# Mean and variance of seven of nine token blocks moved from VectorE to ScalarE in the last superblock of a hybrid decoder step

## The chip, the cores and the metric

The kernel runs on one core of a Trainium2 chip. The metric is the device time of one execution in microseconds (us); for the kernel before it is the median of three runs. A profile of one further execution gives the times of the single instructions. TensorE (PE), VectorE (DVE), ScalarE (ACT), GpSimd (POOL) and SyncE (SP) each work through a queue of their own, in order, and meet through semaphores.

## The reference

One inference step of a two-layer decoder for 1024 prompt tokens and 64 new tokens, with 1024 features. Layer 0 mixes by sliding-window attention and a gated convolution, layer 1 by pooling and dilated attention. Behind each mixer and each squared-ReLU MLP stands a residual layer norm. What the change touches is the last line of it, the norm behind the MLP of layer 1, whose result is the output y:

```python
def layer_norm(x, g, b):
    xf = x.astype(jnp.float32)
    mu = jnp.mean(xf, axis=-1, keepdims=True)
    var = jnp.mean(jnp.square(xf - mu), axis=-1, keepdims=True)
    return ((xf - mu) * lax.rsqrt(var + LN_EPS) * g.astype(jnp.float32) + b.astype(jnp.float32)).astype(x.dtype)

def squared_relu_mlp(x, w1, w2):
    return jnp.square(jax.nn.relu(x @ w1)) @ w2
...
        x = layer_norm(DEEPNORM_ALPHA * x + squared_relu_mlp(x, mlp_w1[layer], mlp_w2[layer]),
                       ln2_g[layer], ln2_b[layer])
```

## The kernel before, in words

The 1088 tokens lie in nine blocks of 128 rows (the ninth, block 8, has the 64 new tokens), and XT[:, t, :] holds the 1024 features of block t. Matmuls are done on values split into a high and a low part, three matmuls for each product. The MLP runs in eight pieces of 512 hidden features. A piece computes its hidden features (matmuls of L1463, then Relu, Square and Copy on ScalarE, L760 to L766), and then a "superblock" of the down product: `row_super` on TensorE (L1494) and `sums` on VectorE (L1129), which adds each finished half block from PSUM to XT. The superblock of the last piece of a layer is also the one whose sums are followed by the layer norm; its number is R = 19 for the end of the kernel, and it is the only one that the change touches.

**TensorE's order.** `row_super` goes through five sets of blocks: (0, 1), (2, 3), (8), (4, 5), (6, 7). A unit is one half of one block: 512 features in one PSUM bank. Four chunks k of the hidden features are summed; k is the outer loop and the units of a set the inner one, so that all four units of a set end close together. A unit has 12 matmuls; those of block 8 have 8. Before the first matmul of a unit TensorE waits until VectorE has emptied the unit's bank (`r_evac`). Behind the set (4, 5) stand the matmuls of L1546, which add up the two halves of block 8 (with SEL), and wait for its sums.

**VectorE's order** is written out by hand in `norm_super` (L1145): the sums of a set, then `ln_stats` (L952) for its blocks, and so on in NORM_ORDER = (0, 1, 2, 3, 4, 5, 8, 6, 7): sums of (0, 1); norms 0, 1; sums of (2, 3); norms 2, 3; sums of (8) and (4, 5); norms 4, 5; the two copies of L1166 for block 8; sums of (6, 7); norms of 8, 6 and 7. The position p in NORM_ORDER is what the code counts by.

**One norm** in this superblock is, on VectorE, two bn_stats (L958, L959) and a bn_aggr (L960) for mean and variance; a pass over the block, (x - mean) * gain (L965); four instructions on one column, which turn the root into its refined reciprocal (L968 to L974); and a second pass, x * 1/std + bias (L980). ScalarE only takes the root of the variance (`ln_root`, L654 to L658) while VectorE does L965. SP stores a block when its second pass is done (L546).

What comes next on VectorE's queue always stands behind the norm in front of it: there is one queue.

Of the kernel before, what the change touches and what calls it, by code (L numbers as in the profile page):

```python
# [67 lines left out]
U_OIN = U_EOUT  # L68
U_OOUT = U_OIN + 3 * ODD_IN + 12
H_UNITS = 12 * N_HB  # L70

ROW_BASE = [0]
for _r in range(20):
# [21 lines left out]
def build(nc, io):  # L95
# [3 lines left out]
    with ctx:  # L99
        place = [nc.sbuf_base + (-nc.sbuf_base) % 64]  # L100

        def at(name, shape, dtype, offset):
            return nc.alloc_sbuf_tensor_at(name, shape, dtype, offset=offset)
# [6 lines left out]
        def small(name, shape):  # L110
            n = 4
            for s in shape[1:]:
                n *= s
            return at(name, shape, F32, room(n))
# [69 lines left out]
        BNS = small("BNS", [P, 12])  # L184
        MV = small("MV", [P, 2, 2])
        NM = small("NM", [P, 2])
        EPSC = small("EPSC", [P, 1])
        SD = small("SD", [P, 2])
        RS = small("RS", [P, 2])
# [24 lines left out]
        def sem(name):  # L214
            return ctx.enter_context(nc.semaphore(name))
# [3 lines left out]
        xr_in = [sem(f"xr_in{q}") for q in range(5)]  # L219
        x0_in = [sem(f"x0_in{q}") for q in range(5)]  # L220
        tables_in, tables_used, y_ready = sem("tables_in"), sem("tables_used"), sem("y_ready")
        r_mm, r_evac, w_free, packed = sem("r_mm"), sem("r_evac"), sem("w_free"), sem("packed")
        spilled = sem("spilled")
        ident_in, cols_in, kct_in, biasa_in = sem("ident_in"), sem("cols_in"), sem("kct_in"), sem("biasa_in")
# [35 lines left out]
        def turned_back(l, g, k):  # L260

            c = k % ring(l, g)
            return XR[:, c, 0:GROUP[g][1]] if c < 2 else RT[:, c - 2, 0:GROUP[g][1]]

        def rows_of(t):

            return NS if t == N_TILES - 1 else P

        def sums_of(R, t):

            q = [t in tiles for tiles in TILE_SETS].index(True)
            if t == N_TILES - 1:
                return ROW_BASE[R] + 16
            return ROW_BASE[R] + row_units(R, q)[-1][0] + 1

        def row_units(R, q):

            first = SET_UNIT[q] + (2 if R in NORM_SUPER and q == 4 else 0)
            return [(first + 2 * i + n, t, n) for i, t in enumerate(TILE_SETS[q]) for n in range(2)]
# [324 lines left out]
        def _(act):  # L604
# [49 lines left out]
            def ln_root(l, p):  # L654
                n, r = 9 * l + p, rows_of(NORM_ORDER[p])
                act.wait_ge(mv_ready, n + 1)
                act.activation(SD[0:r, n % 2:n % 2 + 1], MV[0:r, n % 2, 1:2], ACT.Sqrt,  # L657
                               bias=EPSC[0:r, :]).then_inc(std_ready, 1)  # L658

# [123 lines left out]
            def mlp(l, name, out):  # L783
                ln_super(2 * l)
                hidden_super(l, 0, 2 * l, (name, out, N_HB - 1))
                with act.Fori(0, N_HB - 1) as i:
                    hidden_super(l, i + 1, None, (name, out, i))
# [106 lines left out]
            act.wait_ge(pt_evac, len(turn))  # L894
            split_high(2, Y, (0, 1, 2), (1,))
            mlp(1, "cache_d_v", "d_vs")
            for p in range(9):
                ln_root(3, p)


        @block.vector
        def _(dve):
# [3 lines left out]
            def link(ins):  # L906

                links[0] += 1
                ins.then_inc(dve_link, 1)
                dve.wait_ge(dve_link, links[0])  # L910
# [41 lines left out]
            def ln_stats(l, p):  # L952
                n, t = 9 * l + p, NORM_ORDER[p]
                r, e = rows_of(t), slice(n % 2, n % 2 + 1)
                dve.wait_ge(r_evac, sums_of(NORM_SUPER[l], t))
                if n >= 2:
                    dve.wait_ge(zn_ready, min(n - 1, 27))
                dve.bn_stats(BNS[0:r, 0:6], XT[0:r, t, 0:512])  # L958
                link(dve.bn_stats(BNS[0:r, 6:12], XT[0:r, t, 512:1024]))  # L959
                dve.bn_aggr(MV[0:r, n % 2, :], BNS[0:r, :]).then_inc(mv_ready, 1)  # L960
                if l == 3:
                    if p == 0:
                        dve.wait_ge(tables_in, 16 * 10)
                    dve.wait_ge(mv_ready, n + 1)
                    link(dve.scalar_tensor_tensor(out=XT[0:r, t, :], in0=XT[0:r, t, :], scalar=MV[0:r, n % 2, 0:1],  # L965
                                                  in1=TG[0:r, 0, :], op0=ALU.subtract, op1=ALU.mult))
                dve.wait_ge(std_ready, n + 1)
                link(dve.reciprocal(RS[0:r, e], SD[0:r, e]))  # L968

                link(dve.scalar_tensor_tensor(out=NW[0:r, e], in0=MV[0:r, n % 2, 1:2], scalar=EPS, in1=RS[0:r, e],  # L970
                                              op0=ALU.add, op1=ALU.mult))
                link(dve.scalar_tensor_tensor(out=NW[0:r, e], in0=NW[0:r, e], scalar=-0.5, in1=RS[0:r, e],
                                              op0=ALU.mult, op1=ALU.mult))
                link(dve.scalar_tensor_tensor(out=RS[0:r, e], in0=NW[0:r, e], scalar=1.5, in1=RS[0:r, e],  # L974
                                              op0=ALU.add, op1=ALU.mult))
                if l < 3:
                    dve.scalar_tensor_tensor(out=NM[0:r, e], in0=MV[0:r, n % 2, 0:1], scalar=-1.0, in1=RS[0:r, e],
                                             op0=ALU.mult, op1=ALU.mult).then_inc(rs_ready, 1)
                else:
                    dve.scalar_tensor_tensor(out=XT[0:r, t, :], in0=XT[0:r, t, :], scalar=RS[0:r, e], in1=TG[0:r, 1, :],  # L980
                                             op0=ALU.mult, op1=ALU.add).then_inc(y_ready, 1)

            def ln_residual(l, t):

# [141 lines left out]
                    if g and j:  # L1126
                        split_low(1, Y, (g - 1,), (0,))

            def sums(base, R, q, add=True):  # L1129

                for v, t, n in row_units(R, q):
                    dve.wait_ge(r_mm, base + (v + 1))
                    dve.tensor_tensor(XT[:, t, 512 * n:512 * n + 512], XT[:, t, 512 * n:512 * n + 512],  # L1133
                                      bank(row_bank(q, t, n, R not in (0, 1, 11))), ALU.add).then_inc(r_evac, 1)
# [6 lines left out]
            def freed(base, k):  # L1141

                dve.wait_ge(w_free, base + (k + 1))

            def norm_super(R, t0):  # L1145

                l, base = NORM_SUPER.index(R), ROW_BASE[R]
                sums(base, R, 0)
                ln_stats(l, 0)
                ln_stats(l, 1)  # L1150
                sums(base, R, 1)
                ln_stats(l, 2)
                ln_stats(l, 3)
                sums(base, R, 2)
                sums(base, R, 3)
                ln_stats(l, 4)
                if t0 is not None:
                    freed(3 * R, 0)
                    w_high(t0)
                ln_stats(l, 5)  # L1160
                if t0 is not None:
                    freed(3 * R, 1)
                    w_high(t0 + 1)
                for n in range(2):
                    dve.wait_ge(r_mm, base + 15 + n)
                    dve.tensor_copy(XT[:, N_TILES - 1, 512 * n:512 * n + 512], bank(4 + n)).then_inc(r_evac, 1)  # L1166
                if t0 is not None:
                    freed(3 * R, 2)
                    w_high(t0 + 2)
                sums(base, R, 4)  # L1170
                if t0 is not None:
                    w_high(t0 + 3)
                for p in range(6, 7 if l < 3 else 9):
                    ln_stats(l, p)

            def out_first(l):

# [61 lines left out]
            def mlp(l):  # L1239
                hidden_low(l, 0, 2 * l)  # L1240
                down_super(l, 0)
                hidden_low(l, 1, None)
                with dve.Fori(1, N_HB - 1) as i:
                    down_super(l, i)
                    hidden_low(l, i + 1, None)
                if l == 0:
                    dve.wait_ge(tables_in, 16 * 5)
                    dve.scalar_tensor_tensor(out=TG[:, 1, :], in0=TG[:, 1, :], scalar=ALPHA, in1=TG[:, 0, :],
                                             op0=ALU.mult, op1=ALU.add).then_inc(tables_used, 1)
                norm_super(9 + 10 * l, None if l else T_OIN)  # L1250

            split_low(1, Y, (2,), (0,))
            dve.wait_ge(stored_a, 16 * 18)
# [191 lines left out]
            out_first(1)  # L1445
            norm_super(11, T_MLP[1])
            mlp(1)


        @block.tensor  # L1450
        def _(pe):
# [42 lines left out]
            def row_super(base, R, t0, w_base, src, chunk, ready, pack, hidden=None):  # L1494
# [3 lines left out]
                for q, tiles in enumerate(TILE_SETS):  # L1498
                    ready(q)
                    if q == 2:  # L1500
                        pe.wait_ge(packed, pack)
                    for k in range(4):
                        if q == 0:
                            pe.wait_ge(w_split, w_base + (t0 + k + 1))
                        if norm is not None and norm < 3 and (q, k) in ((3, 1), (3, 2), (3, 3), (4, 0)):
                            p = 0 if q == 3 and k == 1 else 1 if k == 2 else 2 if k == 3 else 3
                            ln_back(norm, 0, (2 * p, 2 * p + 1))
                        for v, t, n in row_units(R, q):
                            b = row_bank(q, t, n, R not in (0, 1, 11))
                            if k == 0:  # L1510
                                if q == 0:
# [26 lines left out]
                                                 start=(k == 0 and i == 0), stop=(k == 3 and i == len(pairs) - 1))  # L1538
                            if k == 3:
                                last.then_inc(r_mm, 1)  # L1540
                        if q == 4 and k < 3:
                            last.then_inc(w_free, 1)
                    if norm is not None and q == 3:
                        pe.wait_ge(r_evac, base + 10)
# [487 lines left out]
```

## Time and profile before

| | us |
|---|---|
| median of 3 runs | 2477.61 (2476.06 to 2480.05) |
| the profiled execution | 2482.34 |
| its span, first to last instruction | 2480.5 |
| TensorE busy, whole span | 2395.8 (97%) |
| VectorE busy, whole span | 1028.9 (41%) |
| ScalarE busy, whole span | 605.8 (24%) |

Times in the trace are microseconds from the start of the span. A row of a timeline gives the start, the duration, the engine, the line, what is written from what, and the count of instructions merged in it. Instructions of one engine overlap a little at their ends (the next starts before the last result is written), so the distance between two starts, and not the duration, says what an instruction costs in a chain on one engine. Shares over the whole span say nothing of the last stage, which begins at about 2412 us.

### The profile page before, as it was taken

Reading aid. Unit: us, or ns where it says so; the run is one execution under the profiler, and the core shown is the slowest. Engines: PE = TensorE matmul, PEld = TensorE weight load, DVE = VectorE, ACT = ScalarE, POOL = GpSimd, SP = SyncE. Lnnn points to the kernel's source line nnn. Section 1 sums busy time; section 2 is a strip of 40 time slices with the busy share of each in tenths; the row PEclk is TensorE's granted clock in tenths of the full one; section 3 lists DMA queues with packets and bytes.
Section 4 is the critical chain, followed back from the end, with each engine's and each line's share of the span. In section 5 each row is a group of like instructions: output and inputs, shape, how many; then the busy total and the mean of one; then the engine's idle time right before and its main releaser. Section 6 shows DMA issues by size and latency. Waiting matters only on the chain.

```text
span 2480.5 us, 35489 instructions
## 1 busy us (share of the span) xinstructions
PE 2395.8 (97%) x14110; PEld 2132.6 (86%) x14110; DVE 1028.9 (41%) x2084; ACT 605.8 (24%) x1280; POOL 481.2 (19%) x222
## 2 busy tenths in 40 slices
PE   8999999999999999999999888999999999999996
PEld 7888888898998998998999555688899899898895
DVE  3555666632222222226723655456622222222228
ACT  1223205220120220223300466515121121121120
POOL 2101212121121122113511100112221221121130
PEclk9999999999999999999999999999999999999998
DMA  5101321231232232232311566642242231241241
GB/s 181 61 18 35 117 67 63 74 122 66 83 111 74 84 98 82 90 101 85 115 44 68 212 230 230 255 41 74 70 128 68 75 127 62 73 135 62 73 135 72
DMA packets 69726, 245.81 MB, mean 99 GB/s; under 512 B 25584, under 2 KB 30320, under 8 KB 61040
## 3 DMA queue, kind: packets, MB, share of 16 engines
q1 hardware_dynamic: 52944, 173.68, 20.6%
q10 hardware_dynamic: 16688, 70.83, 9.5%
q8 instruction: 65, 1.06, 0.2%
q14 instruction: 29, 0.24, 0.0%
HBM read 230.33 MB, written 81.97 MB: 126 GB/s over the span
## 4 chain that ended last, share of the span: by engine, by line
PE 87%; DVE 7%; ACT 3%; issue 2%; DMA 1%; POOL 1%; SPq 0%; ACTq 0%; DVEq 0%
PE PS L1463 45%; PE PS L1537 34%; ACT SMB L805 1%; PE PS L1794 1%; PE PS L1768 1%; DVE XT L1133 1%; DMA WR<-in_w 1%; PE PS L1485 1%; PE PS L1807 1%; POOL WS L558 1%; PE PS L1782 1%; PE PS L1833 1%; PE PS L1582 1%; PE PS L1607 1%; DVE BNS L958 1%
## 5 line engine op out<-in xcount | busy, mean ns | idle before, releaser
L1463 PE MATMUL PS<-XS,WS 128*128 128x384 f32 (+1 forms) x7056 | 1190.7, 328 | 14.5 <-DVE XS L919 11.3
L1463 PEld LDWEIGHTS PS<-XS,WS 128*128 128x128 f32 x7056 | 1167.0, 189 | 29.4 <-issue 18.9
L558 POOL TENSOR_TENSOR WS<-WR,WS 128x1024 fp32r<-128x1024 f32 x178 | 436.8, 2454 | 1825.8 <-DVE WS L934 1054.7
L1537 PE MATMUL PS<-WS,HID 128*128 128x512 f32 x3072 | 703.7, 389 | 0.0
L1537 PEld LDWEIGHTS PS<-WS,HID 128*128 128x128 f32 x3072 | 575.7, 188 | 119.1 <-issue 0.5
L1133 DVE TENSOR_TENSOR XT<-XT,PS 128x512 f32<-128x512 f32 x360 | 236.9, 686 | 372.7 <-PE PS L1537 372.5
L760 ACT ACTIVATE RT<-PS 128x384 f32<-128x384 f32 (+1 forms) x192 | 91.2, 475 | 1098.5 <-PE PS L1463 1098.5
L1212 DVE TENSOR_TENSOR HID<-ST,HID 128x384 fp32r<-128x384 f32 (+1 forms) x192 | 108.4, 564 | 578.5 <-ACT HID L766 578.5
L1537 PE MATMUL PS<-WS,XS 128*128 128x512 f32 x768 | 179.9, 393 | 4.2 <-DVE XT L1133 4.0
L1537 PEld LDWEIGHTS PS<-WS,XS 128*128 128x128 f32 x768 | 144.3, 189 | 35.3 <-DVE XT L1133 5.0
L934 DVE CAST WS<-WR 128x1024 fp32r<-128x1024 f32 x112 | 82.5, 738 | 107.6 <-DMA WR<-in_w 57.8
L764 ACT ACTIVATE ST<-RT 128x384 f32<-128x384 f32 (+1 forms) x192 | 97.7, 509 | 7.8
L766 ACT ACTIVATE HID<-ST 128x384 fp32r<-128x384 f32 (+1 forms) x192 | 97.9, 510 | 6.1
L1537 PE MATMUL PS<-WS,PK 128*128 128x512 f32 x320 | 75.8, 389 | 0.0
L1537 PEld LDWEIGHTS PS<-WS,PK 128*128 128x128 f32 x320 | 60.1, 188 | 12.5
L657 ACT ACTIVATE SD<-MV,EPSC 128x1 f32<-128x1 f32 (+1 forms) x36 | 10.7, 297 | 240.1 <-DVE MV L960 240.1
L929 DVE CAST WS<-WR 128x1024 fp32r<-128x1024 f32 x66 | 51.6, 782 | 32.8 <-DMA WR<-in_w 24.6
L691 ACT ACTIVATE VD<-PS 128x384 f32<-128x384 f32 x8 | 3.9, 493 | 159.8 <-PE PS L1554 159.8
L1768 PE MATMUL PS<-KTD,Y 64*128 64x512 f32 (+3 forms) x192 | 39.6, 517 | 2.2 <-DVE MND L1370 0.9
L1485 PE MATMUL PS<-IDN,XT 128*128 128x128 f32 x216 | 31.9, 282 | 9.3 <-ACT XR L640 9.2
L569 POOL TENSOR_TENSOR XS<-XR,XS 128x384 fp32r<-128x384 f32 (+1 forms) x20 | 21.8, 1112 | 96.3 <-ACT XS L645 96.3
L1485 PEld LDWEIGHTS PS<-IDN,XT 128*128 128x128 f32 x216 | 25.9, 143 | 15.7 <-ACT XR L640 12.1
(182 smaller groups left out, 1356.0 us busy)
## 6 DMA issues: line engine op xcount, KB each, us to landing
WR<-in_w SPq DMA_DIRECT2D x178, 512.0 KB, 3.5
out_d_ks<-in_cache_d_k ACTq DMA_DIRECT2D x96, 340.0 KB
out_d_vs<-in_cache_d_v ACTq DMA_DIRECT2D x96, 340.0 KB
KC<-in_kt SPq DMA_DIRECT2D x16, 1024.0 KB, 10.7
VCD<-in_cache_d_v SPq DMA_DIRECT2D x16, 1024.0 KB, 6.9
TG<-in_rows SPq DMA_DIRECT2D x10, 512.0 KB, 5.7
XT<-in_xt SPq DMA_DIRECT2D x4, 1024.0 KB, 8.3
TH<-in_th SPq DMA_DIRECT2D x4, 1024.0 KB, 11.0
```

What stands on the lines that cost most here:

```text
L558: pool.tensor_tensor(WS[:, slot, 1, :], WR[:, raw, :], WS[:, slot, 0, :].bitcast(F32), ALU.subtract).then_inc(w_split, 1)
L760: act.activation(RT[:, u % 2, 0:gw], bank(4 + u % 2, gw), ACT.Relu).then_inc(h_evac, 1)
L764: act.activation(ST[:, u % 2, 0:gw], RT[:, u % 2, 0:gw], ACT.Square).then_inc(h_sq, 1)
L766: act.activation(HID[:, 0, j, c0:c0 + gw], ST[:, u % 2, 0:gw], ACT.Copy).then_inc(hid_hi, 1)
L929: dve.tensor_copy(WS[:, t % NSLOT, 0, :], WR[:, t % NRAW, :]).then_inc(w_hi, 1)
L934: dve.tensor_copy(WS[:, t % NSLOT, 0, :], WR[:, t % NRAW, :]).then_inc(w_hi, 1)
L1133: dve.tensor_tensor(XT[:, t, 512 * n:512 * n + 512], XT[:, t, 512 * n:512 * n + 512], bank(row_bank(q, t, n, R not in (0, 1, 11))), ALU.ad ...
L1212: dve.tensor_tensor(HID[:, 1, j, c0:c0 + gw], ST[:, u % 2, 0:gw], HID[:, 0, j, c0:c0 + gw].bitcast(F32), ALU.subtract).then_inc(hid_ready, 1)
L1463: last = pe.matmul(out[:, 0:gw], WS[:, slot, a, (off + k) * P:(off + k + 1) * P], src[:, b, k, c0:c0 + gw], start=(n == 0), stop=(n == 3 * ...
L1485: last = pe.transpose(PS[:, back_bank(k), tt * P:tt * P + P], XT[:, 3 * g + tt, k * P:k * P + P], IDN[:, :])
L1537: last = pe.matmul(bank(b), rows, WS[:, (t0 + k) % NSLOT, f, 512 * n:512 * n + 512], start=(k == 0 and i == 0), stop=(k == 3 and i == len( ...
L1768: last = pe.matmul(bank(2 * (u % 2) + h, nk * P), Y[rows, 4 + c, qb * P:qb * P + P], KTD[rows, c, k * P:(k + nk) * P], start=True, stop=True)
```

## The change

In the last superblock only:

- For positions 1 to 7 (blocks 1, 2, 3, 4, 5, 8, 6) ScalarE computes mean and variance: a pass Identity with scale -1/1024 whose sum is the negative mean, a pass Square with the mean as bias whose sum is 1024 times the variance, a Copy that divides one column, and the root. Each waits for the one before it by a semaphore. Positions 0 and 8 keep bn_stats on VectorE.
- VectorE waits for mean and root of such a block before its first pass, and then does what it did before.
- TensorE runs the sets behind the first unit by unit (k is the inner loop).
- VectorE takes sums and norm block by block, and block 8 is normed before the sums of block 6.

```diff
+BY_SCALAR = (1, 2, 3, 4, 5, 6, 7)
...
+        JK = at("JK", [P, 1024], F32, o_xs)
...
             mlp(1, "cache_d_v", "d_vs")
+            def last_stats(p):
+                n, t = 27 + p, NORM_ORDER[p]
+                r, e = rows_of(t), slice(n % 2, n % 2 + 1)
+                i = BY_SCALAR.index(p)
+                act.wait_ge(r_evac, sums_of(19, t))
+                if p >= 2:
+                    act.wait_ge(y_ready, p - 1)
+                act.activation(JK[0:r, :], XT[0:r, t, :], ACT.Identity, scale=-1.0 / D_MODEL, accum_out=NMU[0:r, e])\
+                   .then_inc(sum_ready, 1)
+                act.wait_ge(sum_ready, 2 * i + 1)
+                act.activation(JK[0:r, :], XT[0:r, t, :], ACT.Square, bias=NMU[0:r, e], accum_out=SQ[0:r, e])\
+                   .then_inc(sum_ready, 1)
+                act.wait_ge(sum_ready, 2 * i + 2)
+                act.activation(VV[0:r, e], SQ[0:r, e], ACT.Copy, scale=1.0 / D_MODEL).then_inc(mean_ready, 1)
+                act.wait_ge(mean_ready, i + 1)
+                act.activation(SD[0:r, e], VV[0:r, e], ACT.Sqrt, bias=EPSC[0:r, :]).then_inc(std_ready, 1)
...
             for p in range(9):
-                ln_root(3, p)
+                (last_stats if p in BY_SCALAR else last_root)(p)
...
+            def last_norm(p):
+                n, t = 27 + p, NORM_ORDER[p]
+                r, e = rows_of(t), slice(n % 2, n % 2 + 1)
+                if p in BY_SCALAR:
+                    mean, var, op = NMU[0:r, e], VV[0:r, e], ALU.add
+                    dve.wait_ge(mean_ready, BY_SCALAR.index(p) + 1)
...
+                if p in BY_SCALAR:
+                    dve.wait_ge(std_ready, n + 1)
+                link(dve.scalar_tensor_tensor(out=XT[0:r, t, :], in0=XT[0:r, t, :], scalar=mean,
+                                              in1=TG[0:r, 0, :], op0=op, op1=ALU.mult))
...
             mlp(1)
+            base = ROW_BASE[19]
+            sums(base, 19, 0)
+            last_norm(0)
+            last_norm(1)
+            for q, t, p in ((1, 2, 2), (1, 3, 3), (2, 8, None), (3, 4, 4), (3, 5, 5)):
+                sums(base, 19, q, t)
+                if p is not None:
+                    last_norm(p)
+            for n in range(2):
+                dve.wait_ge(r_mm, base + 15 + n)
+                dve.tensor_copy(XT[:, N_TILES - 1, 512 * n:512 * n + 512], bank(4 + n)).then_inc(r_evac, 1)
+            last_norm(6)
+            sums(base, 19, 4, 6)
+            last_norm(7)
+            sums(base, 19, 4, 7)
+            last_norm(8)
...
-                    for k in range(4):
+                    tail = norm == 3 and q > 0
+                    for k, units in [(k, [u]) for u in row_units(R, q) for k in range(4)] if tail else \
+                            [(k, row_units(R, q)) for k in range(4)]:
```

What `last_norm` does behind the first pass (reciprocal, the two steps of refinement, the second pass, `y_ready`) is as in `ln_stats`.

## Rows read from the trace of the kernel before

**Rows 1.** Windows of the last stage: length, busy time (instructions) by engine, granted clock, DMA.

```profile
2421.00:2433.60 12.60, 12.60 (x58) 10.42 (x57) 11.96 (x22) 0.59 (x2) 0.00 (x0) 1.00 0.10 42
...
2459.30:2477.46 18.16, 1.77 (x8) 1.13 (x6) 17.43 (x34) 0.89 (x3) 0.00 (x0) 0.65 0.21 72
```

**Rows 2.** Timeline of VectorE, last stage: start, duration, line, tile, count, idle before.

```profile
2421.04 2.73 DVE L1133 TENSOR_TENSOR XT<-XT,PS 128x512 f32<-128x512 f32 x4 [4.50 <-PE PS L1537]
2423.80 0.69 DVE L958 BATCH_NORM_STATS2 BNS<-XT 128x6 f32<-128x512 f32 x1
...
2425.12 0.21 DVE L960 BATCH_NORM_AGGREGATE MV<-BNS 128x2 f32<-128x12 f32 x1
...
2428.75 0.69 DVE L958 BATCH_NORM_STATS2 BNS<-XT 128x6 f32<-128x512 f32 x1
...
2430.31 1.29 DVE L965 SCALAR_TENSOR_TENSOR XT<-XT,MV,TG 128x1024 f32<-128x1024 f32 x1
2431.63 0.16 DVE L968 RECIPROCAL RS<-SD 128x1 f32<-128x1 f32 x1
...
2432.41 1.28 DVE L980 SCALAR_TENSOR_TENSOR XT<-XT,RS,TG 128x1024 f32<-128x1024 f32 x1
2433.61 2.47 DVE L1133 TENSOR_TENSOR XT<-XT,PS 128x512 f32<-128x512 f32 x4
2436.12 0.69 DVE L958 BATCH_NORM_STATS2 BNS<-XT 128x6 f32<-128x512 f32 x1
...
2445.85 3.67 DVE L1133 TENSOR_TENSOR XT<-XT,PS 128x512 f32<-128x512 f32 x6
2449.55 0.69 DVE L958 BATCH_NORM_STATS2 BNS<-XT 128x6 f32<-128x512 f32 x1
...
2459.28 1.28 DVE L1166 COPY XT<-PS 128x512 f32<-128x512 f32 x2
...
2462.86 0.68 DVE L958 BATCH_NORM_STATS2 BNS<-XT 64x6 f32<-64x512 f32 x1
...
2472.52 0.69 DVE L958 BATCH_NORM_STATS2 BNS<-XT 128x6 f32<-128x512 f32 x1
...
2476.18 1.28 DVE L980 SCALAR_TENSOR_TENSOR XT<-XT,RS,TG 128x1024 f32<-128x1024 f32 x1
```

**Rows 3.** Timeline of ScalarE, last stage: the first of nine roots.

```profile
2425.37 0.30 ACT L657 ACTIVATE SD<-MV,EPSC 128x1 f32<-128x1 f32 x1 [11.74 <-DVE MV L960]
```

**Rows 4.** Timeline of ScalarE in the attention of layer 1: passes with a sum.

```profile
1395.02 1.28 ACT L805 ACT_TABLE_LOAD   x1
1397.58 1.15 ACT L805 ACTIVATE SMB<-SMB,MND 128x1024 f32<-128x1024 f32 x1 [1.28 <-DVE MND L1370]
1398.64 0.19 ACT L805 ACTIVATION_READ_ACCUMULATOR SMB<-SMB,MND 128x1 f32 x1
1398.73 1.13 ACT L805 ACTIVATE SMB<-SMB,MND 128x1024 f32<-128x1024 f32 x1
```

**Rows 5.** ScalarE by line and form, whole span: count, busy us, mean ns of one.

```profile
L764 ACT ACTIVATE ST<-RT 128x384 f32<-128x384 f32 x128 | 67.5, 527 | 5.8
...
L764 ACT ACTIVATE ST<-RT 128x320 f32<-128x320 f32 x64 | 30.2, 472 | 2.0
L651 ACT ACTIVATE XT<-XT,NM,RS 128x1024 f32<-128x1024 f32 x24 | 29.9, 1246 | 18.8 <-DVE NM L977 18.8
...
L711 ACT ACTIVATE ES<-DS 128x4 f32<-128x4 f32 x17 | 3.5, 207 | 45.0 <-DVE DS L1077 45.0
...
L657 ACT ACT_TABLE_LOAD x2 | 2.6, 1283 | 0.0
```

**Rows 6.** Timeline of TensorE, last stage.

```profile
2411.97 21.95 PE L1537 MATMUL PS<-WS,HID 128*128 128x512 f32 x96
...
2437.39 11.04 PE L1537 MATMUL PS<-WS,HID 128*128 128x512 f32 x48
...
2449.58 11.49 PE L1537 MATMUL PS<-WS,HID 128*128 128x512 f32 x48
```

More of the change, by code:

```diff
@@ L186, in build @@
         NM = small("NM", [P, 2])
+        NMU = small("NMU", [P, 2])
+        VV = small("VV", [P, 2])
+        SQ = small("SQ", [P, 2])
+        JK = at("JK", [P, 1024], F32, o_xs)
         EPSC = small("EPSC", [P, 1])
@@ L221, in build @@
         tables_in, tables_used, y_ready = sem("tables_in"), sem("tables_used"), sem("y_ready")
+        sum_ready, mean_ready = sem("sum_ready"), sem("mean_ready")
         r_mm, r_evac, w_free, packed = sem("r_mm"), sem("r_evac"), sem("w_free"), sem("packed")
@@ L263, in turned_back, with n_by_vector @@
             return XR[:, c, 0:GROUP[g][1]] if c < 2 else RT[:, c - 2, 0:GROUP[g][1]]
+        def n_by_vector(p):
+            return sum(i not in BY_SCALAR for i in range(p))
         def rows_of(t):
@@ L273, in sums_of @@
                 return ROW_BASE[R] + 16
-            return ROW_BASE[R] + row_units(R, q)[-1][0] + 1
+            return ROW_BASE[R] + max(v for v, tile, n in row_units(R, q) if tile == t) + 1
         def row_units(R, q):
@@ L896, in _, with last_root @@
             mlp(1, "cache_d_v", "d_vs")
+            def last_stats(p):
[14 more added lines that the diff above has]
+                act.activation(SD[0:r, e], VV[0:r, e], ACT.Sqrt, bias=EPSC[0:r, :]).then_inc(std_ready, 1)
+            def last_root(p):
+                n, r = 27 + p, rows_of(NORM_ORDER[p])
+                e = slice(n % 2, n % 2 + 1)
+                act.wait_ge(mv_ready, 27 + n_by_vector(p) + 1)
+                act.activation(SD[0:r, e], MV[0:r, n % 2, 1:2], ACT.Sqrt, bias=EPSC[0:r, :]).then_inc(std_ready, 1)
             for p in range(9):
-                ln_root(3, p)
+                (last_stats if p in BY_SCALAR else last_root)(p)
         @block.vector
@@ L960, in ln_stats @@
                 dve.bn_aggr(MV[0:r, n % 2, :], BNS[0:r, :]).then_inc(mv_ready, 1)
[L961 to L966, printed above, removed]
                 dve.wait_ge(std_ready, n + 1)
@@ L975, in ln_stats @@
                                               op0=ALU.add, op1=ALU.mult))
-                if l < 3:
-                    dve.scalar_tensor_tensor(out=NM[0:r, e], in0=MV[0:r, n % 2, 0:1], scalar=-1.0, in1=RS[0:r, e],
-                                             op0=ALU.mult, op1=ALU.mult).then_inc(rs_ready, 1)
-                else:
-                    dve.scalar_tensor_tensor(out=XT[0:r, t, :], in0=XT[0:r, t, :], scalar=RS[0:r, e], in1=TG[0:r, 1, :],
-                                             op0=ALU.mult, op1=ALU.add).then_inc(y_ready, 1)
+                dve.scalar_tensor_tensor(out=NM[0:r, e], in0=MV[0:r, n % 2, 0:1], scalar=-1.0, in1=RS[0:r, e],
+                                         op0=ALU.mult, op1=ALU.mult).then_inc(rs_ready, 1)
@@ new lines, in last_norm @@
+            def last_norm(p):
[4 more added lines that the diff above has]
+                    dve.wait_ge(mean_ready, BY_SCALAR.index(p) + 1)
+                else:
+                    mean, var, op = MV[0:r, n % 2, 0:1], MV[0:r, n % 2, 1:2], ALU.subtract
+                    dve.wait_ge(r_evac, sums_of(19, t))
+                    dve.wait_ge(zn_ready, 27)
+                    dve.bn_stats(BNS[0:r, 0:6], XT[0:r, t, 0:512])
+                    link(dve.bn_stats(BNS[0:r, 6:12], XT[0:r, t, 512:1024]))
+                    dve.bn_aggr(MV[0:r, n % 2, :], BNS[0:r, :]).then_inc(mv_ready, 1)
+                    dve.wait_ge(mv_ready, 27 + n_by_vector(p) + 1)
+                if p == 0:
+                    dve.wait_ge(tables_in, 16 * 10)
+                if p in BY_SCALAR:
+                    dve.wait_ge(std_ready, n + 1)
+                link(dve.scalar_tensor_tensor(out=XT[0:r, t, :], in0=XT[0:r, t, :], scalar=mean,
+                                              in1=TG[0:r, 0, :], op0=op, op1=ALU.mult))
+                dve.wait_ge(std_ready, n + 1)
+                link(dve.reciprocal(RS[0:r, e], SD[0:r, e]))
+                link(dve.scalar_tensor_tensor(out=NW[0:r, e], in0=var, scalar=EPS, in1=RS[0:r, e], op0=ALU.add, op1=ALU.mult))
+                link(dve.scalar_tensor_tensor(out=NW[0:r, e], in0=NW[0:r, e], scalar=-0.5, in1=RS[0:r, e],
+                                              op0=ALU.mult, op1=ALU.mult))
+                link(dve.scalar_tensor_tensor(out=RS[0:r, e], in0=NW[0:r, e], scalar=1.5, in1=RS[0:r, e],
+                                              op0=ALU.add, op1=ALU.mult))
+                dve.scalar_tensor_tensor(out=XT[0:r, t, :], in0=XT[0:r, t, :], scalar=RS[0:r, e], in1=TG[0:r, 1, :],
+                                         op0=ALU.mult, op1=ALU.add).then_inc(y_ready, 1)
@@ L1127, in _, with sums @@
                         split_low(1, Y, (g - 1,), (0,))
-            def sums(base, R, q, add=True):
+            def sums(base, R, q, only=None):
                 for v, t, n in row_units(R, q):
+                    if only not in (None, t):
+                        continue
                     dve.wait_ge(r_mm, base + (v + 1))
@@ L1156, in norm_super @@
                 ln_stats(l, 4)
-                if t0 is not None:
-                    freed(3 * R, 0)
-                    w_high(t0)
+                freed(3 * R, 0)
+                w_high(t0)
                 ln_stats(l, 5)
-                if t0 is not None:
-                    freed(3 * R, 1)
-                    w_high(t0 + 1)
+                freed(3 * R, 1)
+                w_high(t0 + 1)
                 for n in range(2):
@@ L1166, in norm_super @@
                     dve.tensor_copy(XT[:, N_TILES - 1, 512 * n:512 * n + 512], bank(4 + n)).then_inc(r_evac, 1)
-                if t0 is not None:
-                    freed(3 * R, 2)
-                    w_high(t0 + 2)
+                freed(3 * R, 2)
+                w_high(t0 + 2)
                 sums(base, R, 4)
[L1171 to L1174, printed above, removed]
+                w_high(t0 + 3)
+                ln_stats(l, 6)
             def out_first(l):
@@ L1249, in mlp @@
                                              op0=ALU.mult, op1=ALU.add).then_inc(tables_used, 1)
-                norm_super(9 + 10 * l, None if l else T_OIN)
+                if l == 0:
+                    norm_super(9, T_OIN)
             split_low(1, Y, (2,), (0,))
@@ L1507, in row_super @@
                             ln_back(norm, 0, (2 * p, 2 * p + 1))
-                        for v, t, n in row_units(R, q):
+                        for v, t, n in units:
                             b = row_bank(q, t, n, R not in (0, 1, 11))
@@ L1540, in row_super @@
                                 last.then_inc(r_mm, 1)
-                        if q == 4 and k < 3:
+                        if q == 4 and k < 3 and not tail:
                             last.then_inc(w_free, 1)
```

## The prediction

> **What bounds the kernel now.** Over the whole span TensorE is busy 97% of the time, and a change to VectorE's or ScalarE's work would be worth nothing there. But the change touches only the last stage, so I read that stage alone: first the windows by engine, then VectorE's timeline, then what ScalarE and TensorE do beside it. From 2421.00 to 2433.60 us VectorE is busy 11.96 of 12.60 us; from 2459.30 to 2477.46 it is busy 17.43 of 18.16 us, while TensorE has only 1.77 us left to do [rows 1]. VectorE starts its first sums at 2421.04, after its last idle time of any size (4.50 us, waiting for TensorE), and ends its last pass at 2476.18 + 1.28 = 2477.46 [rows 2]; the last store takes the remaining 3.04 us of the span. So the end is set by 56.42 us of VectorE's queue without a gap. ScalarE is busy 0.59 us in the first of those windows [rows 1]. The idea of the change is plain from this; the question is whether ScalarE's work lies beside VectorE's or in line with it.
>
> What the 56.42 us consist of [rows 2]: 20 sums and copies of half a block, which take 2.76 (2421.04 to 2423.80), 2.51 (2433.61 to 2436.12), 3.70 (2445.85 to 2449.55) and 3.58 us (2459.28 to 2462.86), together 12.55; and nine norms, 56.42 - 12.55 = 43.87 us, or 4.87 each (the second: 2428.75 to 2433.61, 4.86).
>
> **What the change removes.** For seven blocks the two bn_stats and the bn_aggr leave VectorE: 2430.31 - 2428.75 = 1.56 us each [rows 2]. What stays of a norm, from the start of the first pass to the next instruction, is 2433.61 - 2430.31 = 3.30 us.
>
> **What it adds: ScalarE's chain for one block.** Four instructions, each waiting for the end of the one before, so here ends count and not starts.
> - The Square pass has 1024 elements, a bias column and a sum. Its nearest row is the pass of L805, also 1024 elements, a bias column and a sum: it starts at 1397.58 and its sum is read out by 1398.64 + 0.19 = 1398.83, which is 1.25 us [rows 4].
> - The Identity pass has no column operand, and no row shows it at 1024. L764 takes 527 ns at 384 and 472 ns at 320 elements [rows 5], 0.86 ns for an element; extended by 640 elements this is 1.08 us, and the read-out ends 0.10 us behind its pass in [rows 4] (1398.83 against 1398.73): 1.18. From above it is bounded by L651 with two column operands, 1.246 us [rows 5], and 0.10: 1.35. From below by 1.08, were the read-out free. I take 1.17, nearest to L764, which has the same operands.
> - Copy on one column: L711, on four columns, takes 207 ns [rows 5]; I take 0.21, with the root's 0.30 [rows 3] as the upper end.
> - The root: 0.30 us [rows 3].
> - Three handovers between them. The root starts at 2425.37 when bn_aggr had ended at 2425.12 + 0.21 = 2425.33, and L968 starts 0.03 us behind the end of L965 (2430.31 + 1.29 to 2431.63) [rows 2, 3]: 0.03 us each, 0.09.
>
> Together L = 1.17 + 1.25 + 0.21 + 0.30 + 0.09 = 3.02 us. Lower end, with both passes without read-out (1.08 + 1.15) and 0.19 for the Copy: 2.81. Upper end, with 1.35 for both passes and 0.30 for the Copy: 3.39. These three are estimates from the rows named.
>
> The Trainium skill ("ScalarE: Activation LUTs", What ACT_TABLE_LOAD costs) gives an ACTIVATE 186 ns, 0.833 ns for an element and 93 ns for each column operand. By that the passes are 1.04 and 1.13 us and L some 0.1 us shorter, so that the sum below would be about 7.5 us instead of 8.1; the page has no price for the read-out, and L805's 1.15 us in this trace is slightly above its figure.
>
> **Beside or in line.** ScalarE may start a block only when that block's sums are in XT. VectorE issues the sums of a block directly before `last_norm` of the same block, and `last_norm` begins with the wait for ScalarE. Between the two VectorE's queue holds nothing else. So for blocks 2, 3, 4, 5, 8 (behind the two copies) and 6 VectorE stands still for the whole of L: the 1.56 us of its own work are replaced by 3.02 us of waiting and two handovers. Behind that wait are queued the sums of all later blocks, so nothing else catches up. Only block 1 is different: its sums are made with those of block 0, ScalarE starts on it behind the root of block 0 (2425.67) and ends at about 2425.70 + 3.02 = 2428.72, and VectorE comes to it at 2428.75. There the passes are hidden.
>
> **The sum.** New length of VectorE's chain: 12.55 for sums and copies; 6 x 0.08, since ScalarE must wait for the end of the second sum and not only its issue (the four sums end 2.47 us behind 2433.61, their starts are some 0.6 us apart and one takes 0.69); 4.95 for the first norm (2423.80 to 2428.75); 3.30 for block 1; 6 x (0.03 + 3.02 + 0.03 + 3.30) = 38.28; 4.94 for the last norm (2472.52 to 2477.46) [rows 2]. That is 64.50 us against 56.42, **8.1 us more**. With L at its ends: 6 x (2.81 - 3.02) gives 6.8, and 6 x (3.39 - 3.02) with 0.37 for block 1, no longer hidden, gives 10.7.
>
> **What costs nothing, and its cover.** TensorE: a unit of 12 matmuls takes 11.04 / 4 = 2.76 us in either order, since the same matmuls run [rows 6]. Units now end earlier, but VectorE is later than TensorE everywhere: it reaches the sums of block 2 at 2432.05, whose units end by 2428.4 (72 of the 96 matmuls that take 21.95 us from 2411.97). Later TensorE waits for VectorE: the third unit of the last set needs the bank that block 5's first sum frees at about 2457. It then ends its last unit at 2457 + 2 x 2.76 = 2462.5; VectorE asks for block 6 at about 2471.6, 9 us later. Even at 1.2 GHz from there on, half of the granted 1.00 of [rows 1], the two units would end at 2468. The stores lie further apart than before; the last is alone on its queue as it was, with the same 3.04 us. Norming block 8 earlier moves work within the same queue.
>
> **How this stands to the runs.** The profiled execution took 2482.34 us, of which 1.84 lie around its span, and is 4.7 us above the median of 2477.61. I carry the difference over: 2477.61 + 8.1 = **2485.7 us**; a profile of the changed kernel would have its last pass on VectorE end near 2485.5.
>
> **Rivals.**
> - *ScalarE's passes run beside VectorE's work* and the kernel becomes faster. Place: the wait at the head of `last_norm`. It would need the statistics of each block to be ready when VectorE arrives, as for block 1. Price: 7 x 1.56 = 10.9 us less; TensorE's last unit at 2461.07 [rows 6], one sum (0.69) and the last norm (4.94) allow no more than about 10.8 either. Time: 2467 us. In line, the sign turns only where L is below 3.02 - 8.1 / 6 = 1.67 us, little more than one pass with its read-out. Against it: the order of the queue. Chance 0.05.
> - *The passes are much shorter than their rows*, L below 2.5, and the difference falls under 0.2% (5.0 us, about what a measurement of this kernel can tell from no change). Two passes at 0.86 ns for an element, the slope of [rows 5] with no fixed part at all, are 1.76 us, and with root, Copy and handovers L would be 2.36: 8.1 - 6 x 0.66 = 4.1 us, 2481.7. For it speaks that no row has Identity at this size with a sum; against it [rows 4]. Chance 0.06.
> - *The functions need different tables.* A load holds ScalarE from 1395.02 to 1397.58, 2.56 us [rows 4]. Two for each of six blocks in line would add 31 us: 2516. Against it: the root's line has two loads in its 36 uses [rows 5], although Square, Identity and Copy run between the roots in every layer. The Trainium skill (the same page, Table sets) counts copy and identity among the functions in every set and says nothing of Square beside the root. Chance 0.03.
>
> **How the numbers follow.** The forecast has 0.86. The range takes the bounds of L, 2484.4 to 2488.3, and the spread of the runs around their median (-1.55, +2.44): 2482.9 to 2490.7. It leaves out the rivals (0.14) and little more. Slower by over 0.2%: 0.86 + 0.03 = 0.89; within 0.2%: 0.06; faster: 0.05.
>
> **What the profile would show.** VectorE idle before the first pass (the line of `last_norm`'s first scalar_tensor_tensor), released by ScalarE's root, six times some 3.1 us; ScalarE's four instructions of one block within 3.0 us, a pass with its read-out at 1.2; TensorE idle for 1 to 3 us before a unit of the last set, released by VectorE's sum. Wrong would be the whole account if VectorE showed no such idle time, and its size if L is outside 2.8 to 3.4.

## The result and the profile after

The changed kernel takes 2485.98 us (median of 7 runs, 2481.92 to 2489.27) against 2478.14 us for the kernel before (7 runs, 2475.66 to 2480.77): a ratio of 1.003, 95% interval 1.002 to 1.0041. It is slower by 7.8 us. The forecast was 2485.7 us.

The profiled execution of the changed kernel took 2487.76 us with a span of 2485.9 us. Its timeline on VectorE in the last superblock (start, duration, line, tile, count, idle time before and who ended it), the answer to [rows 2]:

```profile
2418.43 2.73 DVE L1189 TENSOR_TENSOR XT<-XT,PS 128x512 f32<-128x512 f32 x4 [5.18 <-PE PS L1607]
2421.08 0.69 DVE L1017 BATCH_NORM_STATS2 BNS<-XT 128x6 f32<-128x512 f32 x1
...
2425.94 1.28 DVE L1025 SCALAR_TENSOR_TENSOR XT<-XT,NMU,TG 128x1024 f32<-128x1024 f32 x1
...
2429.23 1.28 DVE L1189 TENSOR_TENSOR XT<-XT,PS 128x512 f32<-128x512 f32 x2
2433.64 1.29 DVE L1025 SCALAR_TENSOR_TENSOR XT<-XT,NMU,TG 128x1024 f32<-128x1024 f32 x1 [3.13 <-ACT SD L923]
...
2436.94 1.28 DVE L1189 TENSOR_TENSOR XT<-XT,PS 128x512 f32<-128x512 f32 x2
2441.35 1.28 DVE L1025 SCALAR_TENSOR_TENSOR XT<-XT,NMU,TG 128x1024 f32<-128x1024 f32 x1 [3.13 <-ACT SD L923]
...
2476.64 1.27 DVE L1189 TENSOR_TENSOR XT<-XT,PS 128x512 f32<-128x512 f32 x2
2477.95 0.69 DVE L1017 BATCH_NORM_STATS2 BNS<-XT 128x6 f32<-128x512 f32 x1
...
2481.62 1.28 DVE L1034 SCALAR_TENSOR_TENSOR XT<-XT,RS,TG 128x1024 f32<-128x1024 f32 x1
```

The first passes at 2433.64 and 2441.35 carry a bracket that no first pass of the kernel before has (one of them is in [rows 2], at 2430.31): VectorE stood idle for 3.13 us until ScalarE's root (L923). The pass at 2425.94, that of block 1, has none. The view of who waited for whom, from 2421.1 us on, counts them: engine and line, released by, us in total, times, longest.

```profile
DVE XT L1025 <- ACT SD L923: 18.8, 6, 3.1
...
PE PS L1607 <- DVE XT L1189: 0.9, 1, 0.9
```

ScalarE's timeline for block 2, the first of the six blocks in line, the answer to [rows 3]:

```profile
2430.54 1.06 ACT L915 ACTIVATE JK<-XT 128x1024 f32<-128x1024 f32 x1 [4.73 <-DVE XT L1189]
2431.51 0.18 ACT L915 ACTIVATION_READ_ACCUMULATOR JK<-XT 128x1 f32 x1
2431.72 1.15 ACT L918 ACTIVATE JK<-XT,NMU 128x1024 f32<-128x1024 f32 x1
2432.78 0.18 ACT L918 ACTIVATION_READ_ACCUMULATOR JK<-XT,NMU 128x1 f32 x1
2433.00 0.20 ACT L921 ACTIVATE VV<-SQ 128x1 f32<-128x1 f32 x1
2433.23 0.29 ACT L923 ACTIVATE SD<-VV,EPSC 128x1 f32<-128x1 f32 x1
2438.25 1.06 ACT L915 ACTIVATE JK<-XT 128x1024 f32<-128x1024 f32 x1 [4.72 <-DVE XT L1189]
```

Block 2's second sum ends at 2429.23 + 1.28 = 2430.51; ScalarE works from 2430.54 to 2433.52, 2.98 us; it has idled for 4.73 us before this block and idles for 4.72 us before the next one (2438.25). Each of the two engines waits for the other. And TensorE, the answer to [rows 6]:

```profile
2434.78 11.04 PE L1607 MATMUL PS<-WS,HID 128*128 128x512 f32 x48
2445.99 1.98 PE L1616 MATMUL PS<-XT,SEL 128*128 128x512 f32 x4 [0.17 <-DVE XT L1189]
2447.41 6.03 PE L1607 MATMUL PS<-WS,HID 128*128 128x512 f32 x24
2454.29 5.73 PE L1607 MATMUL PS<-WS,HID 128*128 128x512 f32 x24 [0.86 <-DVE XT L1189]
```

The measure used from here on is **the chain**: from the start of VectorE's first sum in the last superblock to the end of its last pass. Before it was 56.42 us (2421.04 to 2477.46); now it is 2482.90 - 2418.43 = 64.47 us, 8.05 more. It is sharper than the time: a second profiled execution of the changed kernel gave 64.50 us, while the point at which the stage begins lay between 2413.84 and 2423.84 us in the ten profiled executions of this study, although the work ahead of it is the same in all of them. So the two profiled spans differ by only 5.4 us: the stage of the changed kernel happened to begin 2.61 us earlier. No run was made to move that start, but the traces show what goes along with it, TensorE's granted clock in the work ahead. Windows of 20 us of the kernel before and of the execution whose stage began first (2413.84, the run with TensorE's old order below), columns as in [rows 1]:

```profile
120.00:140.00 20.00, 17.48 (x96) 14.69 (x96) 13.11 (x40) 4.65 (x13) 4.76 (x2) 0.83 0.25 79
```

```profile
120.00:140.00 20.00, 17.48 (x112) 15.21 (x112) 13.07 (x40) 6.64 (x21) 4.75 (x2) 1.00 0.22 78
```

In the kernel before the granted clock is 0.50 (1.2 GHz) from 134 to 140 us; in the other execution it is 1.00 (2.4 GHz) in the same place, and TensorE gets 112 matmuls done there instead of 96. Ahead of the last stage the clock is below 1.00 in four such windows of the execution that began its stage first (0.91 in each), in seven of the changed kernel's (0.91 in each; 2418.43), in eight of the kernel before (0.83 in this one, 0.91 in the others; 2421.04) and in nine of the last to begin (0.74 in one, 0.91 in the others; 2423.84). None of the other six stands out of this order. Why the clock falls in one execution and not in another stays open.

### The profile page after: what moved, and what is told of

Same layout as the page of the kernel before. It is cut to its first block, busy times and chain, and to the rows that moved or that the text cites. A ratio compares the mean times of both kernels' runs of the same rounds, so it can differ in the third digit from the quotient of the medians.

```text
span 2485.9 us, 35509 instructions
## 1 busy us (share of the span) xinstructions
PE 2393.5 (96%) x14110; PEld 2130.1 (86%) x14110; DVE 1017.5 (41%) x2063; ACT 622.2 (25%) x1315; POOL 479.9 (19%) x222
## 3 DMA queue, kind: packets, MB, share of 16 engines
q8 instruction: 65, 1.06, 0.2%
## 4 chain that ended last, share of the span: by engine, by line
PE 87%; DVE 6%; ACT 3%; issue 1%; DMA 1%; POOL 1%; SPq 0%; ACTq 0%; DVEq 0%
PE PS L1531 45%; PE PS L1607 35%; ACT SMB L816 1%; PE PS L1864 1%; PE PS L1838 1%; PE PS L1553 1%; DMA WR<-in_w 1%; PE PS L1877 1%; POOL WS L569 1%; PE PS L1852 1%; PE PS L1903 1%; PE PS L1652 1%; DVE XT L1189 1%; PE PS L1677 1%; DVE XT L1025 0%
```

## The experiments

The theory (A): the loss is the wait in line, six times ScalarE's 3 us in the place of 1.56 us of bn_stats. The main rivals: the new order of sums and units costs it (B); ScalarE's passes slow down VectorE's instructions beside them (C).

**The new order alone.**

```diff
-BY_SCALAR = (1, 2, 3, 4, 5, 6, 7)
+BY_SCALAR = ()
```

> The changed kernel with no block given to ScalarE: TensorE still runs unit by unit, VectorE takes sums and norm block by block, block 8 is normed ahead of block 6, but mean and variance of all nine blocks are bn_stats on VectorE. Measured by VectorE's chain, from the start of its first sum in the last superblock to the end of its last pass: 56.42 us before, 64.47 us in the changed kernel. Theory A (VectorE waits in line for ScalarE's four instructions): without ScalarE's blocks the chain is 56.2 to 56.6 us, and the time is that of the kernel before within 1 us. Rival B (the new order costs the time: sums in smaller groups, TensorE held up at its banks): the chain stays near 64 us and the time near 8 us above the kernel before.

Measured: chain 56.83 us; time 2479.95 us against 2479.1, ratio 0.9999 (0.999 to 1.0009; the ratios are not the quotients of the two medians). VectorE's timeline shows no idle time, only smaller groups:

```profile
2436.20 1.28 DVE L1189 TENSOR_TENSOR XT<-XT,PS 128x512 f32<-128x512 f32 x2
2437.52 0.69 DVE L1017 BATCH_NORM_STATS2 BNS<-XT 128x6 f32<-128x512 f32 x1
```

Two sums and the step to bn_stats take 1.32 us, where four took 2.51 [rows 2]; such steps make the chain 0.41 us longer than before, somewhat more than the band of the expectation. Rival B falls: the order is worth 0.4 of the 8 us.

**Block 1 alone on ScalarE.**

```diff
-BY_SCALAR = (1, 2, 3, 4, 5, 6, 7)
+BY_SCALAR = (1,)
```

> The changed kernel with ScalarE taking mean and variance of block 1 alone, the one block whose sums are in XT well before VectorE comes to its norm. Theory A: the passes are hidden behind the norm of block 0 and only the 1.56 us of bn_stats and bn_aggr go, so that the chain is 1.5 us shorter than with no block given to ScalarE: 54.7 to 55.0 us. Rival C (ScalarE's passes slow down VectorE's instructions that run at the same time): VectorE's passes of block 0 take more than their 1.28 us, and the gain is smaller.

Measured, in one execution of 2480.49 us: chain 55.28 us, 1.55 below the order alone (the band of the expectation was 0.3 too low, since it stood on 56.4 and not on 56.83). ScalarE's two passes over block 1, and VectorE's passes beside them:

```profile
2424.77 1.04 ACT L915 ACTIVATE JK<-XT 128x1024 f32<-128x1024 f32 x1
...
2425.94 1.16 ACT L918 ACTIVATE JK<-XT,NMU 128x1024 f32<-128x1024 f32 x1
```

```profile
2424.57 1.28 DVE L1025 SCALAR_TENSOR_TENSOR XT<-XT,MV,TG 128x1024 f32<-128x1024 f32 x1
...
2426.67 1.28 DVE L1034 SCALAR_TENSOR_TENSOR XT<-XT,RS,TG 128x1024 f32<-128x1024 f32 x1
2427.87 1.28 DVE L1025 SCALAR_TENSOR_TENSOR XT<-XT,NMU,TG 128x1024 f32<-128x1024 f32 x1
```

VectorE's passes take 1.28 us as in [rows 2], and the pass at 2427.87 follows without idle time. Rival C falls, and this block, whose statistics are ready in time, gains the whole 1.55 us: beside other work the move to ScalarE is worth what it takes away. The other six blocks together then cost 64.47 - 55.28 = 9.19 us, 1.53 each.

**Shorter passes, the same waits.** Both passes run over 64 of the 1024 features, so mean and variance of seven blocks are those of 64 features.

```diff
-                act.activation(JK[0:r, :], XT[0:r, t, :], ACT.Identity, scale=-1.0 / D_MODEL, accum_out=NMU[0:r, e])\
+                act.activation(JK[0:r, 0:64], XT[0:r, t, 0:64], ACT.Identity, scale=-1.0 / 64, accum_out=NMU[0:r, e])\
...
-                act.activation(JK[0:r, :], XT[0:r, t, :], ACT.Square, bias=NMU[0:r, e], accum_out=SQ[0:r, e])\
+                act.activation(JK[0:r, 0:64], XT[0:r, t, 0:64], ACT.Square, bias=NMU[0:r, e], accum_out=SQ[0:r, e])\
...
-                act.activation(VV[0:r, e], SQ[0:r, e], ACT.Copy, scale=1.0 / D_MODEL).then_inc(mean_ready, 1)
+                act.activation(VV[0:r, e], SQ[0:r, e], ACT.Copy, scale=1.0 / 64).then_inc(mean_ready, 1)
```

> The changed kernel with both of ScalarE's passes over 64 of the 1024 features, so that mean and variance of seven blocks come from 64 features only; everything else, all waits included, is as in the changed kernel. ScalarE's four instructions for one block take 2.98 us in the changed kernel; without 2 x 960 elements at some 0.84 ns they take about 1.4 us. Theory A: six waits in line become 1.6 us shorter each, and the chain goes from 64.47 to about 54.9 us, 1.5 us below the kernel before, since 1.4 us of waiting now replace 1.56 us of work. Rival B (the order costs it): the chain stays near 64 us. If only some of the waits count, the chain lies between, by 1.6 us for each.

Measured: chain 54.88 us; time 2477.7 us against 2479.1, ratio 1.0 (0.9989 to 1.001). The first of six idle times, and ScalarE's chain ahead of it:

```profile
2429.44 1.28 DVE L1025 SCALAR_TENSOR_TENSOR XT<-XT,NMU,TG 128x1024 f32<-128x1024 f32 x1 [1.53 <-ACT SD L923]
```

```profile
2427.95 0.26 ACT L915 ACTIVATE JK<-XT 128x64 f32<-128x64 f32 x1 [6.34 <-DVE XT L1189]
...
2429.04 0.29 ACT L923 ACTIVATE SD<-VV,EPSC 128x1 f32<-128x1 f32 x1
```

ScalarE needs 1.38 us instead of 2.98, VectorE waits 1.53 instead of 3.13, and the chain is 64.47 - 54.88 = 9.59 us shorter, which is 6 x 1.60. All six waits count in full, and nothing is left over. That the chain is 1.54 us shorter than before has another reason than the expectation gives: block 1 brings 1.55 us, the six blocks in line only 55.28 - 54.88 = 0.40, and the order costs 0.41. The time does not tell 1.5 us from nothing.

**TensorE's old order under the new order of the others.**

```diff
-                    tail = norm == 3 and q > 0
+                    tail = False
```

> The changed kernel with TensorE's old order in the last superblock (all units of a set in each chunk k) under the new order of VectorE and ScalarE. Theory A: VectorE is later than TensorE everywhere, so the order of TensorE's units changes nothing at the end: the chain stays at 64.2 to 64.8 us, while TensorE waits some microseconds longer before the last set's units and ends later. Rival B (TensorE's order is what costs): the chain falls back towards 56 us.

Measured, in one execution of 2483.34 us: chain 64.66 us. TensorE waits longer and does so off the path:

```profile
2433.26 9.86 PE L1607 MATMUL PS<-WS,HID 128*128 128x512 f32 x42 [1.55 <-DVE XT L1189]
...
2449.89 11.46 PE L1607 MATMUL PS<-WS,HID 128*128 128x512 f32 x42 [3.66 <-DVE XT L1189]
```

It waits 3.66 us here against 0.86, and 1.55 us more ahead of another set; the end does not move beyond 0.2 us. In the changed kernel, running unit by unit buys nothing, since VectorE is late.

**Sums ahead of norms.** VectorE adds up the next block before it norms the current one, so that ScalarE has a block to work on meanwhile. Nothing else is changed. (`copies` are the two copies for block 8, as a function.)

```diff
+            def copies():
+                for n in range(2):
+                    dve.wait_ge(r_mm, base + 15 + n)
+                    dve.tensor_copy(XT[:, N_TILES - 1, 512 * n:512 * n + 512], bank(4 + n)).then_inc(r_evac, 1)
+
             sums(base, 19, 0)
             last_norm(0)
+            sums(base, 19, 1, 2)
             last_norm(1)
-            for q, t, p in ((1, 2, 2), (1, 3, 3), (2, 8, None), (3, 4, 4), (3, 5, 5)):
-                sums(base, 19, q, t)
-                if p is not None:
-                    last_norm(p)
-            for n in range(2):
-                dve.wait_ge(r_mm, base + 15 + n)
-                dve.tensor_copy(XT[:, N_TILES - 1, 512 * n:512 * n + 512], bank(4 + n)).then_inc(r_evac, 1)
+            sums(base, 19, 1, 3)
+            last_norm(2)
+            sums(base, 19, 2)
+            last_norm(3)
+            sums(base, 19, 3, 4)
+            sums(base, 19, 3, 5)
+            last_norm(4)
+            copies()
+            last_norm(5)
+            sums(base, 19, 4, 6)
             last_norm(6)
-            sums(base, 19, 4, 6)
+            sums(base, 19, 4, 7)
             last_norm(7)
-            sums(base, 19, 4, 7)
             last_norm(8)
```

> The changed kernel with VectorE's queue turned: the sums of the next block stand before the norm of the current one, so that ScalarE works on a block while VectorE norms the one before. The same seven blocks on ScalarE, TensorE unit by unit, nothing left out. Theory A (the loss is only the place of the wait): ScalarE's 3.0 us lie beside 3.3 us of norm and 1.2 us of sums; the six idle times of 3.13 us go, and what is left is waiting for TensorE's units (some 2 to 4 us in all) and the last norm. Chain about 50 us against 56.42 and 64.47, time about 6 us below the kernel before and 14 below the changed one. Rival (the passes on ScalarE, or the handovers, cost by themselves): the chain stays above 56 us.

Measured: chain 49.71 us; time 2471.15 us against 2478.88, ratio 0.9969 (0.9957 to 0.998). The changed kernel itself, once more and on the same chip:

> The changed kernel once more, beside the kernels with sums ahead of norms and on the same chip, for a comparison in the same rounds. Chain 64.4 to 64.6 us; the time 8 us above the kernel before, to within 2 us. If the chain is the same and the time is not, the difference lies ahead of the last stage, whose start moves from execution to execution.

Measured: chain 64.50 us; time 2487.47 us, ratio 1.0034 (1.0022 to 1.0045) to the same runs of before. The same passes on the same engines are 15 us apart in the chain and 16 in the time, only by where the sums stand in VectorE's queue. VectorE's idle times are now of another kind:

```profile
2445.74 0.69 DVE L1189 TENSOR_TENSOR XT<-XT,PS 128x512 f32<-128x512 f32 x1 [2.03 <-PE PS L1615]
2448.47 0.69 DVE L1189 TENSOR_TENSOR XT<-XT,PS 128x512 f32<-128x512 f32 x1 [2.04 <-PE PS L1615]
```

VectorE has caught up with TensorE and waits for the two units of block 5; it waits for ScalarE no more. A third idle time, of 0.24 us, is also TensorE's.

**That order, with the blocks chosen for it.** Block 4 goes back to VectorE, which would only wait there, and block 7, the last, goes to ScalarE. The edit is shown against the kernel just above.

```diff
-BY_SCALAR = (1, 2, 3, 4, 5, 6, 7)
+BY_SCALAR = (1, 2, 3, 5, 6, 7, 8)
...
             sums(base, 19, 3, 4)
-            sums(base, 19, 3, 5)
             last_norm(4)
+            sums(base, 19, 3, 5)
```

> As the kernel with sums ahead of norms, but block 4, before whose norm VectorE would wait for the units of TensorE, keeps bn_stats on VectorE, and block 7, the last, gets its mean and variance from ScalarE beside the norm of block 6. Theory A: VectorE's idle times shrink to some 2.3 us and the last norm loses 1.56 us; chain about 47.6 us, 8.8 us below the kernel before. The floor is TensorE's last unit, about 40 us after the first sum, plus one sum, ScalarE's four instructions and 3.3 us of norm. Rival: the last block's wait for ScalarE (3.0 us) is not covered by the norm of block 6 (3.3 us), and the chain is that of the kernel with sums ahead, 50 us, or longer.

Measured: chain 47.60 us; time 2471.35 us against 2478.88, ratio 0.9967 (0.9955 to 0.9979). The one long idle time left, and the end:

```profile
2452.08 1.29 DVE L1025 SCALAR_TENSOR_TENSOR XT<-XT,NMU,TG 128x1024 f32<-128x1024 f32 x1 [1.94 <-ACT SD L923]
...
2463.11 1.28 DVE L1034 SCALAR_TENSOR_TENSOR XT<-XT,RS,TG 128x1024 f32<-128x1024 f32 x1
2464.32 1.28 DVE L1025 SCALAR_TENSOR_TENSOR XT<-XT,NMU,TG 128x1024 f32<-128x1024 f32 x1
...
2466.41 1.28 DVE L1034 SCALAR_TENSOR_TENSOR XT<-XT,RS,TG 128x1024 f32<-128x1024 f32 x1
```

The last block's statistics are ready when the norm of block 6 is done. TensorE's last unit ends here at 2460.13, which is 40.04 us behind the first sum (2420.09), so the floor of the expectation is 40.04 + 0.69 + 2.98 + 3.30 = 47.01 us, and 0.6 us are left above it. The chain is 2.1 us shorter than in the run above; the times of the two, 2471.15 and 2471.35, do not tell them apart, since the start of the stage moves by more. Both beat the kernel before and the changed one.

**Sums ahead of norms, with TensorE's old order.** The edit of TensorE's order from above, on top of the sums ahead of norms.

> The kernel with sums ahead of norms, with TensorE's old order of units in the last superblock. In the changed kernel TensorE's order could not matter, since VectorE was late. Theory A: once VectorE keeps up with TensorE, its order counts: the sums of block 2 can then start only when the whole set (2, 3) is nearly done, VectorE is idle there for some 3.5 us, and the chain is about 52 us instead of 50. Rival: TensorE's order is worth nothing here either, and the chain is the same within 0.5 us.

Measured, in one execution of 2477.88 us: chain 52.0 us, 2.3 more than with units one by one. The wait is where it was expected, before the sums of block 2:

```profile
2431.90 1.37 DVE L1189 TENSOR_TENSOR XT<-XT,PS 128x512 f32<-128x512 f32 x2 [3.29 <-PE PS L1615]
```

The 2.3 us are what is left of it: in return the two waits for block 5's units give way to one of 0.85 us for TensorE and one of 1.78 us for ScalarE. So TensorE's part of the change has a worth, but only once VectorE is early enough to wait for it.

## Why the prediction was right, step by step

- **What bounds the stage.** VectorE's queue was the right chain: in all ten profiled executions the last pass on VectorE, and the last store some 3 us behind it, end the span.
- **In line, not beside.** Six idle times of 3.13 us, all released by ScalarE's root, and none for block 1, as the order of the queue had said. That block 1 stayed hidden was partly luck: ScalarE ends at 2425.80 and VectorE comes at 2425.94, 0.14 us later, and 0.12 of that is what the handover took elsewhere; the forecast had left 0.03. The shorter passes show that each microsecond of ScalarE's chain counts six times; the sums ahead of norms show that the same work, beside VectorE's, leaves no wait for ScalarE.
- **The length L.** 2.98 us against 3.02. Identity with its read-out takes 2431.69 - 2430.54 = 1.15 us (estimate 1.17), Square 1.24 (1.25), Copy 0.20 (0.21), the root 0.29 (0.30). The extension of L764 [rows 5] and the row of L805 [rows 4] were good to 0.02 us. The pass itself, without read-out, takes 1.06 us for Identity and 1.15 for Square. The prices in the Trainium skill ("ScalarE: Activation LUTs", What ACT_TABLE_LOAD costs) give 1.04 and 1.13 us for them, an estimate with which the trace agrees within 0.02 us. What the prediction made of these prices was too much: with the 0.10 us for the read-out from [rows 4], L is 0.05 us shorter and not 0.1, and the sum 7.8 us and not 7.5.
- **The sum.** 64.47 us against 64.50. The terms were less exact than that: from ScalarE's root to VectorE's pass it took 0.12 us (2433.52 to 2433.64) and not 0.03, six times, while the first sums and the first norm took 0.2 us less (2418.43 to 2425.94 is 7.51, against 2.76 + 4.95). L was 0.04 us shorter, six times, and the sums behind the first together some 0.1 us. So 0.54 us too little and about as much too much cancelled: the mechanism was right, the last 0.03 us are luck.
- **TensorE.** Its wait was put at 1 to 3 us; it is 0.86 before the last units, a little under that, and 0.17 before L1616. Its last unit ends at 2454.29 + 5.73 = 2460.02, 41.6 us behind the first sum (forecast 41.5) and before VectorE asks for block 6 at 2468.95. The cover held, and with the old order too, where the wait is 3.66 us.
- **The rivals.** None came. No table load stands between the passes and the roots in ScalarE's timeline, where Identity, Square, Copy and Sqrt follow each other at 0.02 to 0.04 us. The price of that rival was misread: in [rows 4] the load itself takes 1.28 us, and the other 1.28 are put down to VectorE's MND, which was read out at 1397.54, 0.04 us before the pass; twelve loads are then 15.4 us and not 31. What the first rival supposed, passes beside VectorE's work, is what the kernels with sums ahead of norms do; its price of 10.8 us was a bound, and 8.8 us of it (56.42 to 47.60) were reached.

The point forecast lies 0.3 us from the median. That is nearer than the spread of the runs (some 7 us) lets one claim; the chain, 64.50 against 64.47, is the comparison that counts.

## What to carry to other kernels

Work moved to an idle engine gains its full worth only if its input is made early enough: before counting what leaves the busy engine's queue, look at what stands in that queue between the instruction that feeds the other engine and the one that waits for it. If nothing stands there, the other engine's whole chain, handovers included, takes the place of the work removed, and every such block pays it: here 3.13 us for 1.60 (from the end of the sums to the first pass, 2437.48 to 2439.08 in the order alone), and with the short passes 1.53 for 1.60. The remedy is to put the next block's feeding step ahead of the current block's long work, and then to ask again which engine is late.

## What the runs showed of the hardware

- Two passes over 1024 elements with a sum took ScalarE 1.15 and 1.24 us with the read-out; the read-out itself lasts 0.18 us and ends some 0.1 us behind the pass.
- VectorE's pass started 0.12 us behind the end of ScalarE's root, in the changed kernel and in the tuned one (2451.96 to 2452.08), while ScalarE started 0.03 us behind the end of VectorE's sum. VectorE had two semaphores to wait for in that place; ScalarE had two as well, one of them set long before. What makes the difference was not tried.
- Identical work ahead of the last stage ended up to 10 us apart from one execution to the next (2413.84 to 2423.84 us), in the order in which the granted clock had fallen below 1.00 on the way. No run changed the clock, so this is what goes along with the start and not a cause shown by an edit.
